# Modulation weights asked for by SyncE, modulation rounds spread by columns, and a later token-matrix store in a two-layer diffusion step

## The chip, the cores and the metric

One core of one Trainium2 chip. The metric is device microseconds of one execution of the whole program; lower is better.

## The reference, cut to what matters

Two layers, each on 1280 tokens (1024 latent, 256 prompt) of width 1024:

```python
ada = silu(cond) @ w_ada[l] + b_ada[l]            # 1024 x 6144, one row per condition
sh1, sc1, g1, sh2, sc2, g2 = split(ada, 6)
h = x * (1 + sc1) + sh1
z = h @ w_in[l]                                   # 1024 x 2816: hyena | conformer | q | k | v
y = concat(hyena(z), conformer(z), attention(rope(q), rope(k), v)) @ w_out[l]
x = layer_norm(ALPHA * x + g1 * y); h = x * (1 + sc2) + sh2
x = layer_norm(ALPHA * x + g2 * (relu(h @ w_mlp1[l]) ** 2 @ w_mlp2[l]))
```

## The kernel before, in words

Every engine has its own program, in order, tied to the others by counting semaphores. The stage at issue is the input projection, once per layer. The columns of `w_in` come as 22 blocks of 128. The first 18 blocks make z tiles, three for each block: tokens 0 to 511, 512 to 1023 and the prompt's 256 (`q` = 0, 1, 2). `Z_ORDER` numbers the 54 tiles; this number is `at`. Tiles 0 to 17 are the first six blocks, `q` outermost; from tile 18 (`Z_FIRST`) on, each block's three tiles follow one another, so that (n, 2) is tile 3n+2. Blocks 18 to 21 make ten value tiles afterwards.

- **TensorE**, `z_tile` (line 1043): waits for the block, and through `z_evac` for the tile four before to have left its PSUM bank (line 1053), multiplies (24 matmuls), and then runs what `modulation(at)` (line 1070) puts behind this tile. After value tile 0 it turns the last prompt keys (`new_keys(3)`, line 1128), which waits for the copy out of tile 53 (line 1103).
- **Modulation.** The columns of `w_ada` that are not loaded at the start are computed beside the projection in blocks of 512 columns, two *rounds* each: 24 rounds in layer 0 and 16 in layer 1, 8 matmuls a round (line 978), plus one *turn* (line 985) for each block. A round needs 1 MB of weights in `ADW`, which holds one round only, so the next round's weights can be asked for only when the round before has been computed (`ada_used`). `ada_round_at(l, r)` (line 127) says behind which tile round r lies: 3 + 2r in layer 0, 19 + 2r in layer 1. Rounds count from 0.
- **ScalarE** copies each z tile out of PSUM (lines 1764, 1772), stores it, and asks for the weights of the next round in `load_ada` (line 1651, two DMAs a round). In the same program stand the convolutions' loads and stores (`conv_load`, `conv_store`): behind tiles 18, 20, ... 30 and 42 it waits for the convolution that VectorE is computing, stores it and loads the next. For the queries and keys (blocks 10 to 17) it makes the high part of the block before (line 1691, waits for GpSimd's rotation), copies tile (n, 2), and asks for 8 DMAs that swap rows into `ZSW` (`partners`, line 1685). `ZSW` is one buffer.
- **GpSimd** splits every weight block into a high and a low part (`split`, lines 770 and 774) and rotates queries and keys (lines 809 to 813), in one order: split of block n, `split_rotated(n - 17)`, `rotate(n - 16)`.
- **SyncE** loads the weight blocks into `RAW`, two buffers: block b is asked for when block b-2 is split (`load_block`, line 594). Blocks of the next stage (`B_FWD`, "forward blocks" 0, 1, ...) follow the 22. Behind block 7 it waits for the layer's input to be final (`xs_ready`), stores the token matrix `XT` (5.2 MB, line 658), waits for that store, and loads the cached keys and the rotation table (`CKR`, `ROPE`) into the room that it leaves.

Of the kernel before, what the change touches and what calls it, by code (L numbers as in the profile page):

```python
# [2 lines left out]

# [9 lines left out]
DEPTH = 2  # L13
# [7 lines left out]
CHUNKS = [(0, 512), (512, 512), (1024, 256)]  # L21
# [14 lines left out]
B_IN, B_FWD, B_INV, B_OUT, B_MLP, BLOCKS = 0, 22, 39, 48, 56, 120  # L36
# [25 lines left out]
ADA_BLOCKS = [[(0, c) for c in range(OWN, 12)] + [(1, c) for c in range(OWN)], [(1, c) for c in range(OWN, 12)]]  # L62
# [5 lines left out]
Z_ORDER = [(n, q) for q in range(3) for n in range(FIRST_TILES)] + \  # L68
    [(n, q) for n in range(FIRST_TILES, Z_V) for q in range(3)]
Z_FIRST = 3 * FIRST_TILES  # L70
# [30 lines left out]
def spot_of(t):  # L101

    return {8: 6144}.get(t, spot(t))
# [20 lines left out]
    return max(x for x in range(at - 6, at) if down_bank(x) == down_bank(at)) + 1  # L124


def ada_round_at(l, r):

    return (3 if l == 0 else Z_FIRST + 1) + 2 * r


def ada_turn_at(l, b):
    return ada_round_at(l, 2 * b + 1) + 1
# [75 lines left out]
def program(nc, ins, consts, outs):  # L209
# [20 lines left out]
    def place(name, shape, dtype, offset):  # L230
        return nc.alloc_sbuf_tensor_at(name, shape, dtype, offset=offset)
# [24 lines left out]
    ADW = place("ADW", [128, 2, 2, 512], F32, ADW_O)  # L256
# [157 lines left out]
    with ExitStack() as ctx:  # L414
# [3 lines left out]
        def signal(name, per_layer=0, start=0):  # L418
            return Signal(ctx.enter_context(nc.semaphore(name)), per_layer, start)
# [7 lines left out]
        ada_in = signal("ada_in", 2 * ADA_MAX * 32)  # L427
        ada_used = signal("ada_used", 2 * ADA_MAX, OWN)
# [20 lines left out]
        h_ready = signal("h_ready", 48, 24)  # L449
# [122 lines left out]
        def column_block(w, l, j):  # L572

            return w[l].rearrange("(k p) n -> p k n", p=128)[:, :, bass.ts(j, 128)]
# [9 lines left out]
        def dft_columns(part, j):  # L584
            return dft_d[part].rearrange("(k p) n -> p k n", p=128)[:, :, j * 128:(j + 1) * 128]
# [7 lines left out]
        def _(sp):  # L593
            def load_block(l, b, source, view3):

                p = b % 2
                sp.wait_ge(blk_ready.sem, blk_ready.at(l, b - 1))
                to = RAW[:, p, :]
                if view3:
                    to = RAW[:, p, :].rearrange("p (k n) -> p k n", k=source.shape[1])  # L600
                sp.dma_start(to, source).then_inc(raw_in[p].sem, 16)
# [44 lines left out]
            layer_vectors(0)  # L646
            for l in range(DEPTH):

                for n in range(ZT):
                    if l or n > 1:  # L650
                        load_block(l, B_IN + n, column_block(w_in, l, COLUMNS[n]), True)
                    if l and n == 3:
                        layer_vectors(l)
                    if n == 7:

                        sp.wait_ge(xs_ready.sem, xs_ready.at(l, 0))
                        for half in range(2):
                            sp.dma_start(x_d[:, 4 * half:4 * half + 4, :], XT[:, 4 * half:4 * half + 4, :])\
                              .then_inc(x_spilled.sem, 16)
                        sp.wait_ge(h_ready.sem, h_ready.at(l, 0))  # L660
                        sp.wait_ge(x_spilled.sem, x_spilled.at(l, 2 * 16))
                        sp.dma_start(CKR[:], cache_k[0, l].rearrange("(t p) m d -> p t (m d)", p=128))\
                          .then_inc(ck_in.sem, 16)
                        sp.dma_start(ROPE[:], rope_d).then_inc(rope_in.sem, 16)
                for j in range(ST):
                    for part in range(2):
                        load_block(l, B_FWD + 2 * j + part, dft_columns(part, j), True)
                load_block(l, B_FWD + 16, dftp_d, False)

# [57 lines left out]
                for i in range(21):  # L727
                    q, j = i // 7, i % 7
# [12 lines left out]
                with sp.Fori(0, GROUPS) as g:  # L741
                    for e in range(4):
                        b = B_MLP + e
                        p = b % 2
# [739 lines left out]
        def _(act):  # L1484
# [124 lines left out]
            for l in range(DEPTH):  # L1609
# [38 lines left out]
                    act.wait_ge(pads_ready.sem, pads_ready.at(l, u - 5))  # L1648
                    S.activation(CFIN[:, 1, :], CFIN[:, 1, :], ACT.Sigmoid).then_inc(glu_done.sem, 1)

                def load_ada(r):

                    w, c = ADA_BLOCKS[l][r // 2]
                    act.wait_ge(ada_used.sem, ada_used.at(l, r))
                    for p in range(2):
                        k = 4 * (r % 2) + 2 * p
                        act.dma_start(ADW[:, p], w_ada[w].rearrange("(k p) n -> p k n", p=128)
                                      [:, k:k + 2, 512 * c:512 * c + 512]).then_inc(ada_in.sem, 16)

                def modulation(at):  # L1660

                    for b, (w, c) in enumerate(ADA_BLOCKS[l]):
                        for half in range(2):
                            r = 2 * b + half
                            if ada_round_at(l, r) == at:
                                if r + 1 < 2 * len(ADA_BLOCKS[l]):
                                    load_ada(r + 1)
                                if half:
                                    act.wait_ge(ada_used.sem, ada_used.at(l, r + 1))
                                    if b == 0:  # L1670
                                        act.wait_ge(lam_ready.sem, lam_ready.at(l, 1))
                                    S.activation(AROW[:], PS[:, 7, :], ACT.Copy).then_inc(ada_kept.sem, 1)
                        if ada_turn_at(l, b) == at:
                            act.wait_ge(ada_turned.sem, ada_turned.at(l, b + 1))
                            to = ADA[:, 4 * (c - OWN):4 * (c - OWN) + 4, :] if w == l else AD0[:, w, 4 * c:4 * c + 4, :]
                            S.activation(to.rearrange("p t v -> p (t v)"), PS[:, 7, 0:8], ACT.Copy)\
                             .then_inc(ada_placed.sem, 1)
# [75 lines left out]
                for at, (n, q) in enumerate(Z_ORDER):  # L1753
# [20 lines left out]
                    first_tiles(at)  # L1774
                    if at == Z_FIRST - 1:
                        act.wait_ge(h_ready.sem, h_ready.at(l, 0))
                    if at == ada_round_at(l, 0) - 1:
                        load_ada(0)
                    modulation(at)
                    if q == 0 and i > 1:  # L1780
                        store_low(i - 2)
# [76 lines left out]
                for n, (t, kind) in enumerate(STEPS):  # L1858
# [6 lines left out]
                    else:  # L1865
                        act.wait_ge(u_psum.sem, u_psum.at(l, FOLD_AT[t] + 1))
                        at = spot_of(t) + 256
# [275 lines left out]
            l = DEPTH - 1  # L2143
# [570 lines left out]
```

## Time and profile before

| | |
|---|---|
| median of 3 runs | 3796.18 us (3788.06 to 3804.03) |
| profiled execution | 3796.43 us |
| span of its instructions | 3794.4 us |
| mean granted TensorE clock | 0.963 of full speed |
| busy: TensorE, VectorE, GpSimd, ScalarE | 92%, 51%, 35%, 29% of the span |
| mean DMA rate over the span | 97 GB/s |

The span is what the trace shows; the execution's own time is 2.0 us longer. The projection's stretches are about 92 to 417 us (layer 0) and 1966 to 2252 us (layer 1). In a row of the trace "[t <-X]" is the time that the engine sat idle before the instruction, and what ended it; "ACTq" and "SPq" are DMA requests by ScalarE and SyncE.

### The profile page before, as it was taken

The numbers are of one execution on the slowest core, as the hardware profiler recorded it, in microseconds if no ns is written. First come the engines' busy times: TensorE is split into PE (matmuls) and PEld (weight loads), VectorE is DVE, ScalarE is ACT, GpSimd is POOL, SyncE is SP. The second block draws the span as 40 slices with busy tenths as digits, with TensorE's granted clock in tenths as the row PEclk, the third lists the DMA queues.
The fourth block names the chain that finished last, engine by engine and source line by source line (L and its number), as shares of the span: only waits on it lengthen the run. The fifth ranks groups of instructions, "written<-read, shape, count | busy, mean of one in ns | idle before, by whom it ended". The sixth has DMA issues, their size and how long they took to land. (4 is left out here: it accounts for less than half of the span.)

```text
span 3794.4 us, 48305 instructions
## 1 busy us (share of the span) xinstructions
PE 3473.6 (92%) x18386; PEld 2908.7 (77%) x18386; DVE 1949.2 (51%) x2787; ACT 1101.3 (29%) x2020; POOL 1331.2 (35%) x682
## 2 busy tenths in 40 slices
PE   6899997898899999999978899788899999999996
PEld 4677776787788888888867677577777888888885
DVE  3047665875744434444562775387674344344347
ACT  4212244672511111111242113367524111111114
POOL 3337543201533332323354474430125333323232
PEclk8999998999999999999989999899999999999998
DMA  7577646512011111111117664564201111111101
GB/s 255 213 244 230 206 124 171 134 61 81 31 38 45 34 44 35 40 39 34 34 50 252 211 211 155 160 146 120 72 21 45 34 45 34 43 36 39 39 23 56
DMA packets 285270, 368.46 MB, mean 97 GB/s; under 512 B 16887, under 2 KB 203493, under 8 KB 283782
## 3 DMA queue, kind: packets, MB, share of 16 engines
q1 hardware_dynamic: 211586, 212.63, 19.4%
q10 hardware_dynamic: 73476, 152.83, 11.8%
q8 instruction: 159, 2.61, 0.3%
q14 instruction: 49, 0.40, 0.0%
HBM read 275.48 MB, written 81.53 MB: 94 GB/s over the span
## 5 line engine op out<-in xcount | busy, mean ns | idle before, releaser
L770 POOL TENSOR_TENSOR RH<-RAW,ONE 128x1024 fp32r<-128x1024 f32 x200 | 386.9, 1934 | 1529.8 <-PE PS L929 684.5
L929 PE MATMUL PS<-HH,RH 128*128 128x512 f32 (+1 forms) x2744 | 616.1, 368 | 66.7 <-issue 25.7
L774 POOL TENSOR_TENSOR RL<-RAW,RH 128x1024 fp32r<-128x1024 f32 x240 | 578.9, 2415 | 162.3 <-ACT RH L1905 146.6
L929 PEld LDWEIGHTS PS<-HH,RH 128*128 128x128 f32 x2744 | 471.8, 195 | 187.0 <-issue 92.9
L929 PE MATMUL PS<-HL,RH 128*128 128x512 f32 (+1 forms) x2744 | 586.0, 356 | 0.0
L2555 DVE SCALAR_TENSOR_TENSOR XT<-PS,ADA,XT 128x512 f32<-128x512 f32 (+1 forms) x704 | 454.0, 663 | 244.0 <-PE PS L1421 240.4
L929 PE MATMUL PS<-HH,RL 128*128 128x512 f32 (+1 forms) x2744 | 579.1, 353 | 0.0
L929 PEld LDWEIGHTS PS<-HL,RH 128*128 128x128 f32 x2744 | 467.6, 192 | 74.2
L929 PEld LDWEIGHTS PS<-HH,RL 128*128 128x128 f32 x2744 | 460.9, 189 | 70.9
L2080 ACT ACTIVATE RB<-PS 128x512 f32<-128x512 f32 (+1 forms) x192 | 101.0, 526 | 1390.5 <-PE PS L929 1390.5
L2539 DVE TENSOR_TENSOR PS<-PS,RB 128x512 f32<-128x512 f32 (+1 forms) x192 | 117.1, 610 | 745.8 <-ACT RB L2080 745.8
L1421 PE MATMUL PS<-HBH,RH 128*128 128x512 f32 x1024 | 316.8, 391 | 3.7 <-DVE XT L2555 2.4
L1421 PE MATMUL PS<-HBL,RH 128*128 128x512 f32 x1024 | 315.6, 389 | 0.0
L1421 PE MATMUL PS<-HBH,RL 128*128 128x512 f32 x1024 | 315.4, 389 | 0.0
L2421 DVE TENSOR_REDUCE STAT<-PS 128x1 f32<-128x1280 f32 (+1 forms) x160 | 203.6, 1276 | 70.0 <-PE PS L1273 66.6
L1421 PEld LDWEIGHTS PS<-HBH,RH 128*128 128x128 f32 x1024 | 189.5, 188 | 44.9 <-DVE XT L2575 4.7
L1421 PEld LDWEIGHTS PS<-HBL,RH 128*128 128x128 f32 x1024 | 192.2, 188 | 40.4
L1421 PEld LDWEIGHTS PS<-HBH,RL 128*128 128x128 f32 x1024 | 192.2, 188 | 40.2
L2323 DVE SCALAR_TENSOR_TENSOR PS<-CFIN,VEC,PS 128x1024 f32<-128x1024 f32 (+1 forms) x232 | 206.5, 890 | 8.1
L1273 PE MATMUL PS<-KK,QH 128*128 128x512 f32 (+1 forms) x416 | 163.6, 393 | 39.6 <-ACT PB L1959 31.6
L1959 ACT ACTIVATE PB<-PS,STAT 128x1280 f32<-128x1280 f32 (+1 forms) x160 | 183.7, 1156 | 23.7 <-DVE STAT L2421 23.4
L1316 PE MATMUL PS<-V,AT 128*128 128x128 f32 x1344 | 170.4, 281 | 5.8 <-ACT OT L1989 1.3
(264 smaller groups left out, 4535.7 us busy)
## 6 DMA issues: line engine op xcount, KB each, us to landing
RAW<-in_w_mlp_dram SPq DMA_DIRECT2D x128, 512.0 KB, 3.9
ADW<-in_w_ada_dram ACTq DMA_DIRECT2D x80, 512.0 KB, 5.7
RAW<-const_dram SPq DMA_DIRECT2D x52, 512.0 KB, 4.1
RAW<-in_w_in_dram SPq DMA_DIRECT2D x44, 512.0 KB, 4.8
z_scratch<-ZST ACTq DMA_DIRECT2D x40, 256.0 KB, 3.2
x_scratch<-XT SPq DMA_DIRECT2D x4, 2560.0 KB, 12.8
QH<-q_hi SPq DMA_DIRECT2D x32, 320.0 KB, 9.4
QL<-q_lo SPq DMA_DIRECT2D x32, 320.0 KB, 10.6
```

What stands on the lines that cost most here:

```text
L770: nc.gpsimd.tensor_tensor(RH[:, s, :], RAW[:, p, :], ONE[:].broadcast_to([128, 1024]), ALU.mult)\
L774: nc.gpsimd.tensor_tensor(RL[:, s, :], RAW[:, p, :], RH[:, s, :].bitcast(F32), ALU.subtract)\
L929: mm = pe.matmul(out, w[:, s, k * 128:(k + 1) * 128], m(k), start=(n == 0 and k == 0), stop=(n == 2 and k == KT - 1))
L1273: mm = pe.matmul(PSF[:, SCORES[m] + o:SCORES[m] + o + w], qq[:, m, t * 128:(t + 1) * 128], KK[s][:, m, k0 + o:k0 + o + w], start=(x == 0), ...
L1316: mm = pe.matmul(PS[:, 7, 0:128], AT[:, g % 2, k * 128:(k + 1) * 128], V2[s][:, k0 // 128 + k, :], start=(k == 0), stop=(k == nk - 1))
L1421: mm = pe.matmul(PS[:, down_bank(m), 0:tn], w[:, slot(l, b + e), j * 128:(j + 1) * 128], x[:, e, 0:tn], start=(n == 0 and e == 0), stop=(n ...
L1959: S.activation(PB[:, g % 2, m, :kn], PSF[:, SCORES[m]:SCORES[m] + kn], ACT.Exp, bias=STAT[:, g % 4, m:m + 1], accum_out=STAT[:, g % 4, 2 + ...
L2080: S.activation(RB[:, e, :tn], PS[:, e, :tn], ACT.Relu).then_inc(relu_done.sem, 1)
L2323: C.link(V.scalar_tensor_tensor(acc if k < 30 else CFIN[:, 1, at:at + n], CFIN[:, 0, at + k:at + k + n], VEC[:, w:w + 1], acc, ALU.mult, A ...
L2421: V.tensor_reduce(STAT[:, g % 4, m:m + 1], PSF[:, SCORES[m]:SCORES[m] + kn], AX_X, ALU.max, negate=True).then_inc(smax.sem, 1)
L2539: V.tensor_tensor(up, up, RB[:, e, :tn], ALU.mult).then_inc(sq_kept.sem, 1)
L2555: V.scalar_tensor_tensor(x, PS[:, 2 + m % 6, :tn], ADA[:, A_G2 + j, COND[q]:COND[q] + 1], x, ALU.mult, ALU.add).then_inc(m2_evac.sem, 1)
```

## The change

The requests for rounds' weights move from ScalarE to SyncE. There they stand between the weight blocks: ahead of block b, SyncE asks for every round whose predecessor lies behind a tile that must be done before block b's place in the ring comes free (`freed_at`). `spread` puts the rounds at even steps of computed columns, from tile 3 (layer 0) or tile 15 (layer 1) to tile 52. The store of `XT` comes after one or two rounds' requests; the wait for its end, `CKR` and `ROPE` come after block 9 and no longer ahead of block 8. The tiles of the rounds become

```
layer 0: 3 5 7 9 11 13 17 19 21 23 25 27 30 31 34 36 38 40 42 44 46 48 51 52
layer 1: 15 19 21 24 26 28 31 33 36 38 40 43 45 48 50 52
```

```diff
+def spread(l):
+    first, n = (3, 2 * len(ADA_BLOCKS[0])) if l == 0 else (Z_FIRST - 3, 2 * len(ADA_BLOCKS[1]))
+    width = [CHUNKS[q][1] for _, q in Z_ORDER]
+    done = list(itertools.accumulate(width))
+    last = len(width) - 2
+    step = (done[last] - done[first]) / (n - 1)
+    at = [min(k for k in range(first, last + 1) if done[k] >= done[first] + step * r - 1) for r in range(n)]
+    for r in range(n - 2, -1, -1):
+        at[r] = min(at[r], at[r + 1] - 1 - r % 2)
+    return at
...
 def ada_round_at(l, r):
-    return (3 if l == 0 else Z_FIRST + 1) + 2 * r
+    return ADA_AT[l][r]
...
+                rounds_loaded = [0]
+                def load_ada(upto):
+                    while rounds_loaded[0] < 2 * len(ADA_BLOCKS[l]):
+                        r = rounds_loaded[0]
+                        if (ada_round_at(l, r - 1) if r else ada_round_at(l, 0) - 2) > upto:
+                            return
+                        w, c = ADA_BLOCKS[l][r // 2]
+                        if r == 0:
+                            sp.wait_ge(h_ready.sem, h_ready.at(l, 0 if l else -16))
+                        sp.wait_ge(ada_used.sem, ada_used.at(l, r))
+                        for p in range(2):
+                            k = 4 * (r % 2) + 2 * p
+                            sp.dma_start(ADW[:, p], w_ada[w].rearrange("(k p) n -> p k n", p=128)
+                                         [:, k:k + 2, 512 * c:512 * c + 512]).then_inc(ada_in.sem, 16)
+                        rounds_loaded[0] = r + 1
+                def freed_at(b):
+                    return Z_ORDER.index((b - 8, 2)) if b >= 8 else 2 * b - 10
+
                 for n in range(ZT):
+                    load_ada(freed_at(n))
                     if l or n > 1:
                         load_block(l, B_IN + n, column_block(w_in, l, COLUMNS[n]), True)
...
                     if n == 7:
+                        load_ada(13 if l else 8)
                         sp.wait_ge(xs_ready.sem, xs_ready.at(l, 0))
+                        sp.wait_ge(h_ready.sem, h_ready.at(l, 0))
                         for half in range(2):
                             sp.dma_start(x_d[:, 4 * half:4 * half + 4, :], XT[:, 4 * half:4 * half + 4, :])\
                               .then_inc(x_spilled.sem, 16)
-                        sp.wait_ge(h_ready.sem, h_ready.at(l, 0))
+                    if n == 9:
                         sp.wait_ge(x_spilled.sem, x_spilled.at(l, 2 * 16))
                         sp.dma_start(CKR[:], cache_k[0, l].rearrange("(t p) m d -> p t (m d)", p=128))\
                           .then_inc(ck_in.sem, 16)
                         sp.dma_start(ROPE[:], rope_d).then_inc(rope_in.sem, 16)
                 for j in range(ST):
                     for part in range(2):
+                        if 2 * j + part < 4:
+                            load_ada(freed_at(B_FWD + 2 * j + part))
                         load_block(l, B_FWD + 2 * j + part, dft_columns(part, j), True)
...
-                def load_ada(r):
...
                             if ada_round_at(l, r) == at:
-                                if r + 1 < 2 * len(ADA_BLOCKS[l]):
-                                    load_ada(r + 1)
...
-                    if at == ada_round_at(l, 0) - 1:
-                        load_ada(0)
                     modulation(at)
```

## Rows read from the trace of the kernel before

**Rows 1.** TensorE's waits, 90 to 420 us: engine line, waited for, total us, times, longest

```profile
PE PS L978 <- DMA ADW<-in_w_ada_dram: 15.5, 7, 4.2
...
PE PS L1107 <- ACT ZRAW L1772: 1.6, 1, 1.6
```

**Rows 2.** the same, 1990 to 2256 us

```profile
PE PS L978 <- DMA ADW<-in_w_ada_dram: 23.7, 8, 7.4
...
PE PS L1107 <- ACT ZRAW L1772: 2.7, 1, 2.7
```

**Rows 3.** TensorE in order of time, layer 0's value tile 0: start, us, what

```profile
411.46 2.00 PE L1120 MATMUL PS<-RH,HH 128*128 128x512 f32 x8
...
418.67 0.44 PE L1107 MATMUL PS<-IDENT,ZRAW 128*128 128x128 f32 x2 [1.58 <-ACT ZRAW L1772]
```

**Rows 4.** ScalarE in order of time, end of layer 0's projection

```profile
381.35 0.90 ACTq L1657 DMA_DIRECT2D ADW<-in_w_ada_dram  x2
...
382.35 5.10 ACTq L1685 DMA_DIRECT2D ZSW<-ZRAW  x8
...
399.48 1.28 ACT L1691 ACTIVATE ZHI<-ZRAW 128x1280 fp32r<-128x1280 f32 x1 [4.89 <-POOL ZRAW L813]
...
401.06 5.00 ACTq L1685 DMA_DIRECT2D ZSW<-ZRAW  x8
...
417.08 1.27 ACT L1691 ACTIVATE ZHI<-ZRAW 128x1280 fp32r<-128x1280 f32 x1 [7.41 <-POOL ZRAW L813]
```

**Rows 5.** GpSimd in order of time, the same stretch

```profile
392.23 2.38 POOL L809 TENSOR_TENSOR ZSW<-ZSW,ROPE 128x1024 f32<-128x1024 f32 x1 [4.29 <-DMA ZSW<-ZRAW]
...
401.38 2.39 POOL L774 TENSOR_TENSOR RL<-RAW,RH 128x1024 fp32r<-128x1024 f32 x1
...
409.81 2.41 POOL L809 TENSOR_TENSOR ZSW<-ZSW,ROPE 128x1024 f32<-128x1024 f32 x1 [3.12 <-DMA ZSW<-ZRAW]
```

**Rows 6.** ScalarE, then VectorE, in order of time, layer 0's first convolutions

```profile
202.64 1.46 ACTq L1636 DMA_DIRECT2D HYIN<-z_scratch  x3
...
216.15 0.83 ACTq L1618 DMA_DIRECT2D hyena_scratch<-CACC  x2
...
223.77 0.81 DVE L2300 TENSOR_SCALAR PS<-HYIN,VEC 128x512 f32<-128x512 f32 x1 [7.52 <-DMA HYIN<-z_scratch]
```

**Rows 7.** requests for round weights: count, ns of one request (min, median, max)

```profile
L1657 ACTq DMA_DIRECT2D ADW<-in_w_ada_dram x80: 374/490/1768, 101.8 to 2217.5; - x80
```

**Rows 8.** waits of the whole span for the loads of both rings

```profile
POOL ZSW L809 <- DMA ZSW<-ZRAW: 67.5, 16, 8.3
...
DVE PS L2300 <- DMA HYIN<-z_scratch: 61.2, 10, 7.9
```

**Rows 9.** a load of round weights that TensorE waited for: ScalarE, then TensorE

```profile
361.07 0.94 ACTq L1657 DMA_DIRECT2D ADW<-in_w_ada_dram  x2
...
368.71 1.07 PE L978 MATMUL PS<-ADW,CONDS 128*32 128x512 f32 x8 [1.51 <-DMA ADW<-in_w_ada_dram]
```

**Rows 10.** GpSimd in order of time, block 10's split in layer 0

```profile
198.95 2.39 POOL L774 TENSOR_TENSOR RL<-RAW,RH 128x1024 fp32r<-128x1024 f32 x1
```

**Rows 11.** TensorE in order of time, layer 1, after a long wait

```profile
2037.28 1.94 PE L978 MATMUL PS<-ADW,CONDS 128*32 128x512 f32 x8 [7.40 <-DMA ADW<-in_w_ada_dram]
...
2039.15 2.08 PE L929 MATMUL PS<-HH,RH 128*128 128x256 f32 x8
...
2043.93 2.00 PE L929 MATMUL PS<-HH,RH 128*128 128x512 f32 x8
```

**Rows 12.** SyncE, then GpSimd, then ScalarE in order of time, layer 1, tiles 18 to 20

```profile
2031.49 0.38 SPq L662 DMA_DIRECT2D CKR<-in_cache_k_dram  x1
...
2032.43 41.58 SPq L601 DMA_DIRECT2D RAW<-in_w_in_dram  x7
...
2047.34 1.89 POOL L770 TENSOR_TENSOR RH<-RAW,ONE 128x1024 fp32r<-128x1024 f32 x1 [34.12 <-DMA RAW<-in_w_in_dram]
...
2050.55 0.83 ACTq L1618 DMA_DIRECT2D hyena_scratch<-CACC  x2
```

More of the change, by code:

```diff
@@ L1 @@
+import itertools
 import math
@@ L124, in down_free @@
     return max(x for x in range(at - 6, at) if down_bank(x) == down_bank(at)) + 1
+def spread(l):
[8 more added lines that the diff above has]
+    return at
+ADA_AT = [spread(l) for l in range(DEPTH)]
 def ada_round_at(l, r):
-    return (3 if l == 0 else Z_FIRST + 1) + 2 * r
+    return ADA_AT[l][r]
 def ada_turn_at(l, b):
@@ L1649, in gate @@
                     S.activation(CFIN[:, 1, :], CFIN[:, 1, :], ACT.Sigmoid).then_inc(glu_done.sem, 1)
-                def load_ada(r):
[L1653 to L1658, printed above, removed]
                 def modulation(at):
```

## The prediction

> **What bounds the kernel now.** I read first who TensorE waits for in the two stretches of the projection. Weights of modulation rounds are the largest entry that the change touches: 15.5 us in 7 waits in layer 0, 23.7 us in 8 in layer 1, 39.2 us together [rows 1, 2]. It is tempting to call that the gain. But the same view has a second line: at line 1107 TensorE also waits 1.6 and 2.7 us for ScalarE's copy of a z tile, and in order of time this wait comes after the last round: value tile 0 begins at 411.46, the keys' transposes only at 418.67, when tile 53 has been copied [rows 3]. So with all those stalls in it TensorE still arrives early. Something else ends last, and a stall taken away before that point only makes this wait longer.
>
> What that is, the order of time on ScalarE and GpSimd shows. From one high part to the next (399.48 to 417.08) is a closed ring of 17.6 us: high part 1.3, the row-swap requests from 401.06 to 406.06, their landing, the rotation from 409.81, and with its end the next high part [rows 4, 5]. One ring a block, eight blocks a layer; no round weights stand in it. Ahead of it lies a second ring: convolution inputs asked for at 202.64, computed, stored and the next asked for at 216.15; VectorE sits 7.52 us idle for one of these loads [rows 6]. So the stretch from tile 18 to tile 53, 202.64 to 418, is a chain of ScalarE, VectorE, GpSimd and DMA landings, and TensorE keeps step beside it. I take this chain as the bound in both layers.
>
> **The change, part by part.** The profiled execution is 3796.4 us, within 0.3 us of the median, so the sum is made against 3796.4.
>
> *Requests leave ScalarE.* 80 requests at a median 0.49 us are 39 us of ScalarE's requesting [rows 7]. In the ring they stand beside an activation or where ScalarE waits anyway; worth zero. Another effect is worth something: a round's load in the same queue ahead of the row swaps delays them. With one asked for at 381.35 the swaps, all asked for by 387.45, were landed at 392.23, 4.8 us; without one ahead, 406.06 to 409.81, 3.75 us [rows 4, 5]. That is 1.0 us; by the spread of the loads I count two such turns a layer: **-2.0 us in each layer**. Bounds: 0 (the bytes still move) and 8 (every turn). The Trainium skill ("DMA: Bandwidth & Descriptors", section "Issuing engines are not separate DMA queues") speaks against it: requests from either engine run on the same 16 DMA engines and interleave, and a second issuer saves only issue time. By that rule the term is 0 and the sum 4 us higher; the two landings above differ in what lay ahead in one queue, which the rule leaves open.
>
> *Rounds and turns.* Their number is unchanged; 1.07 us a round stays [rows 9]. Moving them costs nothing while the chain covers them.
>
> *Requests on SyncE.* Here the change adds waits. SyncE is in order: a round's weights wait for the weight block ahead, and that for GpSimd's split. Queued behind SyncE's own waits for `ada_used` are only weight blocks whose place in the ring is not free earlier anyway: zero. The other direction costs, in three places. A late load takes 7.6 us from request to use (361.07 to 368.71) [rows 9]; after a long wait the round itself takes 1.9 us, and the next 256-wide tile 4.8 (2039.15 to 2043.93) [rows 11].
>
> 1. Layer 0, round 7 (tile 19). It stands behind block 12's request, which waits for block 10's split, done at 201.3 [rows 10]. `CKR` and `ROPE`, 1.5 MB, now lie among those blocks. Their delay is not in the trace: between 0 and 12 us (CKR, ROPE and a block, 2 MB, took 15.9 us in layer 1, 2031.49 to 2047.34 [rows 12]); I take 1.6, since blocks have slack between splits. Request 203.3, landed 210.9, round 1.9, tile 20 4.8, copy 0.4: 218.0, where ScalarE stored the first convolution at 216.15 [rows 6]. The chain moves **+1.9 us**.
> 2. Layer 0, round 23 (tile 52). By the code it stands behind forward block 2, which waits for the split that ends at 403.8 [rows 5]. Request 404.2, use 411.8, round 1.9, tile 53 4.8, turn 0.8, value tile 0 5.6 (411.46 to the wait that ended at 418.67, less 1.6 [rows 3]): 424.9 instead of 418.67, **+6.2 us**. Before, this last round's load hid behind tiles.
> 3. Layer 1, round 1 (tile 19). It stands behind block 10, block 10 behind the split of block 8, block 8 in SyncE's queue behind the token matrix, whose end was seen at 2031.49 [rows 12]. Plus 2.5 for block 8 (bounds 0 and 15.9 as above; it now has only the store ahead of it), 4.3 for its split, 0.4: request 2038.7. Landing between 7.6 and 15.9 us, with CKR, ROPE and two blocks about; I take 10, nearer the lower, since part of them has landed by then: 2048.7. Round 1.9, tile 20 4.8, copy 0.4: 2055.8, where the convolution's store stood at 2050.55: **+5.3 us** on the chain. The wait of 7.4 us at 2037.28 [rows 11] is thereby not removed but replaced by a longer one.
>
> *Token matrix.* In layer 1 it still starts when its input is final; in layer 0 it starts some 20 us later, beside rounds whose weights had slack: zero, at most one late load.
>
> The sum: layer 0 -2.0 + 1.9 + 6.2 = +6.1; layer 1 -2.0 + 5.3 = +3.3; 3796.4 + 9.4 = **3806 us**. All that is behind the projection waits for TensorE and moves along.
>
> **The rivals.**
> *A, the stalls were the bound.* All 39.2 us go, and five rounds no longer run at 1.9 instead of 1.07: -4. 3796.4 - 43 = 3753. For it: they are the largest waits. Against: the wait at line 1107 comes after them [rows 1 to 3]. Chance 0.06.
> *B, the chain gets shorter.* 16 row swaps cost GpSimd 67.5 us and 10 convolution loads cost VectorE 61.2 [rows 8]. With round weights out of ScalarE's queue each of the 26 could land 1.0 us sooner (the difference above): -26. With my late loads (+13.4) that is 3784, without them 3770; middle 3777. Against: of the two swaps shown one had no round load ahead. Chance 0.17, half of it past the bound for faster.
> *C, no leg gets shorter.* The two -2.0 fall out: 3796.4 + 13.4 = 3810. Requests only change queue, the bytes and their times stay. The section of the Trainium skill named above says the same. Chance 0.12.
> *D, slower: round weights stuck in SyncE's queue.* Place: rounds 7 and 23 in layer 0 and round 1 in layer 1, asked for right behind blocks and tables. If each takes 15.9 us instead of 7.6, 7.6 and 10, that is +8.3, +8.3 and +5.9 more: 3796.4 + 9.4 + 22.5 = 3828. It decides past 0.5% once the three together take about 10 us more than I gave them. For it: 15.9 was seen in just that queue. Against: rounds asked for beside a block took 7.6 [rows 9]. Chance 0.14.
> *E, it does not do what it says*: the even spacing is undone, since late rounds follow GpSimd's splits and not the columns. That is part of the forecast, not beside it.
>
> **How the numbers follow.** Forecast 0.51, A 0.06, B 0.17, C 0.12, D 0.14. The likeliest is mine: 3806. 0.5%, or 19 us, is about what a measurement of this kernel can tell from no change: 3777 and 3815. Faster: A and half of B, 0.14. Slower: D and 0.04 of the forecast's and C's upper ends, 0.18. The rest, 0.68, is the same. The range leaves out A and part of B below, part of D above: 3781 to 3822.
>
> **What would show it.** Right: TensorE's waits for round weights shrink in number but not at tile 19 of layer 1 and tile 52 of layer 0; the ring stays near 17.6 us; the value tiles begin some 6 and 3 us later; ScalarE's requests for `ADW` are gone. Wrong: a ring or convolution turn that is clearly shorter (B), the value tiles 15 us earlier with no wait at line 1107 (A), or SyncE asking for round 23 or round 1 before the split that I name, which would take away the two largest terms.

## The result, and the profile after

The changed kernel took 3826.03 us (median of 5 runs, 3813.43 to 3827.55) against 3798.87 us for the kernel before on the same chip: ratio 1.0071, 95% interval 1.0054 to 1.0087, that is 27 us or 0.7% slower. The forecast was 3806, with a range up to 3822. The profiled execution of the changed kernel took 3821.70 us; its span is 3819.9 us, the mean granted clock 0.959 (before 0.963). The chip read and wrote as much as before (275.48 and 81.53 MB); what changed in the queues is who asked. The page's rows for the two large DMA queues (packets, MB, share of the 16 engines):

```profile
q1 hardware_dynamic: 233346, 254.57, 22.5%
q10 hardware_dynamic: 51716, 110.88, 8.5%
```

Before, they stood at 212.63 and 152.83 MB: 42 MB, the 80 loads of 0.5 MB, went from one queue to the other, so q1 is SyncE's and q10 ScalarE's. First the waits of the whole span (waited for, total us, times, longest):

```profile
POOL ZSW L855 <- DMA ZSW<-ZRAW: 93.4, 16, 16.4
...
DVE PS L2333 <- DMA HYIN<-z_scratch: 73.4, 10, 14.5
...
PE PS L1024 <- DMA ADW<-in_w_ada_dram: 35.6, 10, 16.0
...
PE PS L1031 <- ACT AROW L1707: 27.6, 5, 9.9
```

Against [rows 8] GpSimd waits 26 us longer for row swaps and VectorE 12 us longer for convolution loads. TensorE's waits for round weights, 39.2 us before in [rows 1, 2], hardly fell; they are fewer and longer. The last row is TensorE's wait at the turn for ScalarE's copy of the row. In the kernel before it was small:

```profile
PE PS L985 <- ACT AROW L1672: 1.9, 3, 1.0
```

Second, the end of layer 0's projection, in order of time on ScalarE, SyncE, GpSimd and TensorE. It answers to [rows 3 to 5]:

```profile
410.04 1.27 ACT L1726 ACTIVATE ZHI<-ZRAW 128x1280 fp32r<-128x1280 f32 x1 [9.36 <-POOL ZRAW L859]
...
411.61 5.00 ACTq L1720 DMA_DIRECT2D ZSW<-ZRAW  x8
...
431.03 1.27 ACT L1726 ACTIVATE ZHI<-ZRAW 128x1280 fp32r<-128x1280 f32 x1 [3.47 <-POOL ZRAW L859]
...
414.33 0.37 SPq L619 DMA_DIRECT2D RAW<-const_dram  x1
414.75 1.46 SPq L682 DMA_DIRECT2D ADW<-in_w_ada_dram  x2
...
423.84 2.35 POOL L855 TENSOR_TENSOR ZSW<-ZSW,ROPE 128x1024 f32<-128x1024 f32 x1 [6.63 <-DMA ZSW<-ZRAW]
...
424.69 1.94 PE L1024 MATMUL PS<-ADW,CONDS 128*32 128x512 f32 x8 [4.34 <-DMA ADW<-in_w_ada_dram]
...
437.10 0.38 PE L1153 MATMUL PS<-IDENT,ZRAW 128*128 128x128 f32 x2
```

The ring that took 17.6 us in [rows 4] takes 21.0 here (410.04 to 431.03). GpSimd finishes a split at 414.3, SyncE is thereby free to ask for the next block, and right behind it for 1 MB of round weights. That falls among ScalarE's eight swap requests (411.61 to 416.61). The last swap lands at 423.84, 7.2 us after the last request; in [rows 4, 5] it was 3.75 us. This time, from the eighth request to the start of the rotation that waits for the swaps, is called a leg below.

The other blocks of layer 0 agree. In four of the eight, SyncE asked for round weights 3.1 to 4.3 us behind the first swap request: their legs are 5.4, 6.5, 7.1 and 7.2 us. The other four took 1.9 to 4.0 us.

The same happens to the last convolution load (SyncE, ScalarE, VectorE):

```profile
273.59 9.35 SPq L682 DMA_DIRECT2D ADW<-in_w_ada_dram  x4
...
275.22 2.18 ACTq L1682 DMA_DIRECT2D HYIN<-z_scratch  x3
...
282.77 0.55 DVE L2333 TENSOR_SCALAR PS<-HYIN,VEC 128x256 f32<-128x256 f32 x1 [8.27 <-DMA HYIN<-z_scratch]
```

Before, VectorE waited 4.14 us for this load, and now 8.27:

```profile
277.33 0.55 DVE L2300 TENSOR_SCALAR PS<-HYIN,VEC 128x256 f32<-128x256 f32 x1 [4.14 <-DMA HYIN<-z_scratch]
```

Third, layer 1 around the token matrix (SyncE, TensorE, ScalarE), which answers to [rows 11, 12]:

```profile
2030.52 0.82 SPq L702 DMA_DIRECT2D x_scratch<-XT  x2
2031.38 11.29 SPq L619 DMA_DIRECT2D RAW<-in_w_in_dram  x2
2046.62 0.37 SPq L706 DMA_DIRECT2D CKR<-in_cache_k_dram  x1
...
2053.42 0.37 SPq L619 DMA_DIRECT2D RAW<-in_w_in_dram  x1
2053.83 1.27 SPq L682 DMA_DIRECT2D ADW<-in_w_ada_dram  x2
...
2028.01 1.07 PE L1024 MATMUL PS<-ADW,CONDS 128*32 128x512 f32 x8
...
2062.19 1.94 PE L1024 MATMUL PS<-ADW,CONDS 128*32 128x512 f32 x8 [16.04 <-DMA ADW<-in_w_ada_dram]
...
2069.67 1.24 ACTq L1664 DMA_DIRECT2D hyena_scratch<-CACC  x2
```

Round 0 was done at 2029, so `ADW` was free; round 1 was asked for at 2053.8, some 25 us later, because SyncE stood behind blocks that waited for GpSimd's splits and for the token matrix. TensorE stood still for 16.0 us.

### The profile page after: what moved, and what is told of

The parts are those of the page before. It is cut to its first block and busy times, and to the rows that moved or that the text cites. A ratio compares the mean times of both kernels' runs of the same rounds, so it can differ in the third digit from the quotient of the medians.

```text
span 3819.9 us, 48306 instructions
## 1 busy us (share of the span) xinstructions
PE 3474.6 (91%) x18386; PEld 2912.5 (76%) x18386; DVE 1934.2 (51%) x2787; ACT 1099.8 (29%) x2020; POOL 1331.6 (35%) x682
## 3 DMA queue, kind: packets, MB, share of 16 engines
HBM read 275.48 MB, written 81.53 MB: 93 GB/s over the span
```

## The experiments

Each kernel was timed in five rounds against the kernel before on its chip (medians of before 3795 to 3799 us). The table gives the ratio to before with its 95% interval, and for layer 0's projection, from one profiled execution each, how much more time than before passed in three stretches: from the first projection matmul to the last hyena convolution's store ("conv"), on to the high part before tile 53 ("rings"), on to the end of the value tiles ("tail"). Where two kernels have the same program in layer 0, the three together differed by 1 to 3 us, one stretch by 3.3; smaller differences are not read. The mean granted clock alone does not set the time: the profiled executions of e6 and e8 took 3794.74 and 3794.64 us at 0.960 and 0.966.

| kernel | asks for rounds | ratio | conv | rings | tail |
|---|---|---|---|---|---|
| changed | SyncE | 1.0071 (1.0054 to 1.0087) | +6.4 | +8.5 | +4.4 |
| e1 spread only | ScalarE | 1.0015 (1.0005 to 1.0025) | -0.1 | +2.2 | +6.3 |
| e2 all but spread | SyncE | 1.0108 (1.0090 to 1.0125) | +14.1 | +7.1 | +2.7 |
| e3 late keys only | ScalarE | 1.0019 (1.0007 to 1.0030) | +8.3 | +1.3 | 0.0 |
| e4 all but late keys | SyncE | 1.0102 (1.0085 to 1.0118) | +15.2 | +8.4 | +5.3 |
| e7 SyncE only | SyncE | 1.0130 (1.0113 to 1.0148) | +14.6 | +5.1 | +1.6 |
| e8 all but SyncE | ScalarE | 1.0016 (1.0002 to 1.0031) | -0.8 | +2.3 | +6.5 |
| e5 before, small loads | ScalarE | 0.9971 (0.9957 to 0.9985) | +1.7 | -4.8 | 0.0 |
| e6 changed, small loads | SyncE | 1.0003 (0.9994 to 1.0012) | -2.7 | -2.3 | +4.3 |
| f1 two requests earlier | SyncE | 1.0070 (1.0054 to 1.0086) | +4.3 | +6.8 | +1.0 |
| f2 and held for swaps | SyncE | 1.0058 (1.0043 to 1.0074) | +7.1 | +1.8 | +3.4 |
| f3 layer 1 alone of e8 | ScalarE | 1.0009 (0.9996 to 1.0022) | +0.6 | +0.2 | 0.0 |
| f4 and behind swaps | ScalarE | 1.0018 (1.0006 to 1.0031) | +0.5 | +3.1 | +0.1 |
| g1 | layer 0 SyncE | 1.0047 (1.0030 to 1.0064) | +9.7 | +7.1 | +5.8 |
| g2 | layer 1 SyncE | 1.0023 (1.0012 to 1.0035) | -0.3 | +2.8 | +7.0 |
| g3 turns later | SyncE | 1.0072 (1.0058 to 1.0086) | +5.3 | +8.7 | +5.3 |
| g4 f1 and round 2 | SyncE | 1.0035 (1.0024 to 1.0047) | +5.0 | +5.1 | 0.0 |

**The three parts, alone and in pairs.** e1 is the kernel before with the new tiles, and ScalarE still asks:

```diff
 def ada_round_at(l, r):
-    return (3 if l == 0 else Z_FIRST + 1) + 2 * r
+    return ADA_AT[l][r]
```

> The kernel before with the new tiles for the rounds alone; ScalarE still asks for their weights, and the token matrix is stored as before (in layer 1 the first request waits besides for the layer's input, because round 0 is now ahead of tile 18). Theory (requests of SyncE that come with a weight block, right behind GpSimd's split, slow down the row swaps and convolution loads of the rings): the spacing alone costs only what lies at its end, a last round at tile 52 whose load can be asked for no sooner than behind tile 51, 3 to 6 us in layer 0 and the same or less in layer 1; 3799 plus 3 to 10 is 3802 to 3809, rings of layer 0 near 17.6 us. Rival S (the spacing itself is the loss: turns at tiles 32 and 44 wait 8 to 10 us for ScalarE's row copy, and the last round is at tile 52): nearly all of the 27 us, 3818 to 3826.

Measured: 3805.38 us. The theory holds, and the place is the named one: of layer 0's three stretches only the tail grew by more than equal programs differ by. Round 23 stands directly behind round 22's tile there, and its load does not fit into one tile.

e2 is the changed kernel with the rounds' tiles put back:

```diff
 def ada_round_at(l, r):
-    return ADA_AT[l][r]
+    return (3 if l == 0 else Z_FIRST + 1) + 2 * r
...
-                        if (ada_round_at(l, r - 1) if r else ada_round_at(l, 0) - 2) > upto:
+                        if (ada_round_at(l, r - 1) if r else 13 if l else 1) > upto:
```

> The changed kernel with the rounds put back to tiles 3 + 2r and 19 + 2r; SyncE asks, between the weight blocks, token matrix stored late. Theory: most of the loss is still here, since the requests still come right behind GpSimd's splits: the last row swap of layer 0 takes about 7 us and no longer 3.75, high part of tile 53 8 to 14 us late; without the last round behind tile 53 some 4 us a layer are saved: 3811 to 3822. Rival S (spacing): 3796 to 3803, no leg longer. Rival P (place of the token matrix): as the theory here, told apart by the next two.

Measured: 3836.54 us, above every number named. The sign is the theory's (the spacing is not the loss), the size is not: under SyncE's requests the even spacing saves about 14 us. The extra loss is in "conv", and most of it stands already at the first convolution's store: 8.3 us behind the kernel before, counted from the start of the stretch, where the changed kernel is 1.9 behind. Why was not traced.

e3 is the kernel before with the wait for the store's end and the two tables' loads moved from behind block 7 to behind block 9; the store itself stays where it was, now behind the wait for `h_ready`:

```diff
                         sp.wait_ge(xs_ready.sem, xs_ready.at(l, 0))
+                        sp.wait_ge(h_ready.sem, h_ready.at(l, 0))
...
-                        sp.wait_ge(h_ready.sem, h_ready.at(l, 0))
+                    if n == 9:
                         sp.wait_ge(x_spilled.sem, x_spilled.at(l, 2 * 16))
                         sp.dma_start(CKR[:], cache_k[0, l].rearrange("(t p) m d -> p t (m d)", p=128))\
                           .then_inc(ck_in.sem, 16)
                         sp.dma_start(ROPE[:], rope_d).then_inc(rope_in.sem, 16)
```

> The kernel before with the wait for the token matrix, the cached keys and the rotation table moved behind block 9, and nothing else; ScalarE asks at the old tiles. Theory: the rings are untouched, within 5 us of before: 3794 to 3804; in layer 1 the longest wait for round weights gets shorter or stays, since blocks 8 and 9 no longer stand behind the token matrix. Rival P (a late 1.5 MB of keys and table pushes block 10 and the first convolution): 3806 to 3816, first convolution of layer 1 stored 4 us or more later.

Measured: 3803.87 us, at the edge between the two. All of layer 0's +8.3 stands at its first convolution's store. Ahead of it TensorE waits for round 7, whose weights ScalarE asked for at 185.8, right behind the two tables (182.9 to 184.6):

```profile
196.70 1.93 PE L979 MATMUL PS<-ADW,CONDS 128*32 128x512 f32 x8 [4.98 <-DMA ADW<-in_w_ada_dram]
```

In the kernel before this round came without a wait. e4 is the changed kernel with the reverse of it, and with the store behind round 0's request alone in layer 0:

```diff
-                        load_ada(13 if l else 8)
+                        load_ada(13 if l else 1)
...
-                    if n == 9:
                         sp.wait_ge(x_spilled.sem, x_spilled.at(l, 2 * 16))
```

> The changed kernel with the wait for the token matrix, the cached keys and the rotation table put back ahead of block 8 (and round 0 of layer 0 the only one asked for ahead of the store); SyncE asks, spread rounds. Theory: the loss of layer 0 stays (about 16 us at its last high part), in layer 1 round 1 is still late: 3818 to 3830. Rival P: 10 us or more come back: 3805 to 3814.

Measured: 3831.96 us, above both forecasts, by the ratios 0.31% or 12 us more than the changed kernel. So the later tables cost 7 us where ScalarE asks at the old tiles; where SyncE asks at the new ones, they and the later store save 12 us: the parts do not add up. That left two corners of the table, e7 with SyncE's requests alone (the edits of e2 and e4 in one kernel) and e8 with everything else (e1 and e3 in one kernel):

> SyncE asks, rounds at their old tiles, token matrix, keys and table stored and loaded as before: the one part of the change that no other run has alone. From the runs so far: spread rounds take 14 us off the run with SyncE's requests and the late keys, and the early keys add 9 us to the run with spread rounds. If the parts add up this run is at 3799 + 40 + 9 or so, 3840 to 3855; if the old tiles and the early keys cost through the same wait, 3828 to 3840. Rival (SyncE's requests do no harm alone, only together with one of the others): 3797 to 3806.

> Spread rounds and late keys, ScalarE asks: all of the change but who asks. Theory: the two small losses add up, 3797 + 6 + 7: 3804 to 3814, GpSimd's wait for row swaps stays near 68 us; the difference to the changed kernel, 15 us or more, is then SyncE's. Rival: the two together already make most of the loss, 3818 to 3828.

Measured: e7 3841.36 us, the low end of the forecast for parts that add up; e8 3799.82 us, below its forecast and less than e1 and e3 added. By the ratios SyncE's asking alone costs more than the whole loss, 1.30% or 49 us; spacing and late tables give 22 us of it back. Against e8 the changed kernel loses 0.55%, 21 us, to who asks.

**Are the bytes the cost, or the order?** e5 and e6 load only 64 of 512 columns:

```diff
+                            cn = 512 if r == 0 else 64
-                            sp.dma_start(ADW[:, p], w_ada[w].rearrange("(k p) n -> p k n", p=128)
-                                         [:, k:k + 2, 512 * c:512 * c + 512]).then_inc(ada_in.sem, 16)
+                            sp.dma_start(ADW[:, p, :, 0:cn], w_ada[w].rearrange("(k p) n -> p k n", p=128)
+                                         [:, k:k + 2, 512 * c:512 * c + cn]).then_inc(ada_in.sem, 16)
```

> The kernel before, with every round but each layer's first loading only 64 of its 512 columns (7/8 of those modulation weights are left out; matmuls, requests and waits keep their number). A round's load is then there almost at once. Theory (the rings are the bound, not TensorE's waits for round weights): little comes back, the legs that run beside a round's load and one tail a layer: 3782 to 3796. Rival A of the prediction (the stalls are the bound): 39 us less, 3755 to 3765.

> The changed kernel with the same columns left out. Theory (the loss is the bytes of round weights landing beside row swaps, convolution loads and blocks, and the late landings of rounds that follow a split): the loss all but goes, within 8 us of the run before with small loads, GpSimd's wait for row swaps falls from 93 us to 75 or less. Rival O (the order is the loss: SyncE's program holds blocks and rounds behind one another, and turns wait for ScalarE's row copy, whatever the size): still 15 us or more above the run before with small loads.

Measured: e5 3782.93 us, 11 us less than before: most of rival A's 39 us were never there. e6 is 0.3%, some 12 us, above e5, and stands between the two forecasts. In layer 0 the loss is gone but for the tail of the new spacing. There the swaps were asked for, and landed, in this way (ScalarE, SyncE, GpSimd of e6):

```profile
393.03 5.00 ACTq L1720 DMA_DIRECT2D ZSW<-ZRAW  x8
...
395.78 0.37 SPq L619 DMA_DIRECT2D RAW<-const_dram  x1
396.19 1.43 SPq L683 DMA_DIRECT2D ADW<-in_w_ada_dram  x2
...
402.22 2.35 POOL L855 TENSOR_TENSOR ZSW<-ZSW,ROPE 128x1024 f32<-128x1024 f32 x1 [3.55 <-DMA ZSW<-ZRAW]
```

Requests at the same moments as in the changed kernel, an eighth of the bytes, and the swaps land 4.2 us after the last request and not 7.2. In the four blocks of layer 0 whose legs were 5.4 to 7.2 us, e6 has 3.8 to 4.2. So in layer 0's rings it is the bytes that land among the swaps; for the convolutions the run doesn't tell their bytes from the rounds' later landing. In layer 1 TensorE still waits 13.4 us at tile 19 with loads this small:

```profile
2043.40 1.93 PE L1024 MATMUL PS<-ADW,CONDS 128*32 128x512 f32 x8 [13.38 <-DMA ADW<-in_w_ada_dram]
```

There it is the order. GpSimd's total wait for swaps, 76.5 us, missed the 75 by a little.

Why do ScalarE's own requests not do the same harm? In e8 the block at the same place shows it (ScalarE, GpSimd):

```profile
402.19 5.00 ACTq L1706 DMA_DIRECT2D ZSW<-ZRAW  x8
...
407.94 1.64 ACTq L1678 DMA_DIRECT2D ADW<-in_w_ada_dram  x2
...
410.97 2.34 POOL L828 TENSOR_TENSOR ZSW<-ZSW,ROPE 128x1024 f32<-128x1024 f32 x1 [3.15 <-DMA ZSW<-ZRAW]
```

ScalarE's program puts the round's weights behind the eighth swap (or ahead of the first), never between them; 3.8 us from the last request to the use. Over e8's eight blocks of layer 0 the legs are 1.9 to 4.1 us.

**Moving requests.** f1 moves two requests up in SyncE's program; f2 holds the others back until the block's swaps are landed:

```diff
 ADA_AT = [spread(l) for l in range(DEPTH)]
+ADA_AT[0][22] = 50
...
-                        load_ada(13 if l else 8)
+                        load_ada(15 if l else 8)
```
```diff
                         sp.wait_ge(ada_used.sem, ada_used.at(l, r))
+                        if swaps > 0:
+                            sp.wait_ge(qk_partner.sem, qk_partner.at(l, swaps * 8 * 16))
```

> The changed kernel with two requests moved up in SyncE's program and nothing else: round 22 of layer 0 goes from tile 51 to tile 50, so that round 23 is asked for ahead of forward block 2's wait and not behind it; round 1 of layer 1 is asked for ahead of the token matrix. Theory (a request's place behind a split or the store is a loss of its own): layer 0's value tiles end 4 to 8 us earlier and its last leg of row swaps is back under 5 us; in layer 1 TensorE's wait of 16.0 us at tile 19 goes, the first convolution is stored 6 to 10 us earlier; together 10 to 18 us: 3806 to 3816. Rival (only the sum of bytes matters): 3820 or more.

> The same, and in the stretch of queries and keys SyncE holds a round's weights back until the row swaps of the block are landed. Theory (what lengthens the swaps' legs is a round's weights asked for by the other queue among the eight swaps): no leg over 4.7 us from the last request to the landing, GpSimd's wait for the swaps in layer 0 from 51 us to 38 or less, layer 0's last high part 6 to 10 us earlier than in the changed kernel; rounds come later, which may cost TensorE some waits that are not on the chain: 3798 to 3810. Rival (the rounds' lateness was the loss, the legs follow it): slower than the run beside it, 3815 or more.

Measured: f1 3823.19 us, no gain, against the theory's 10 to 18. It lies in the rival's range, but the rival (only the bytes matter) does not survive g4 below, where one more request is moved and no byte. In layer 0 the tail came back (+1.0 from +4.4). In layer 1 the wait had moved from round 1 to round 2 (SyncE, TensorE, ScalarE of f1):

```profile
2023.50 0.91 SPq L683 DMA_DIRECT2D ADW<-in_w_ada_dram  x2
...
2049.76 14.41 SPq L620 DMA_DIRECT2D RAW<-in_w_in_dram  x4
2064.21 1.34 SPq L683 DMA_DIRECT2D ADW<-in_w_ada_dram  x2
...
2040.44 1.07 PE L1025 MATMUL PS<-ADW,CONDS 128*32 128x512 f32 x8
...
2073.17 1.93 PE L1025 MATMUL PS<-ADW,CONDS 128*32 128x512 f32 x8 [18.14 <-DMA ADW<-in_w_ada_dram]
...
2082.75 0.60 ACT L1800 ACTIVATE ZST<-PS 128x512 f32<-128x512 f32 x1 [18.59 <-PE PS L976]
...
2083.77 0.92 ACTq L1665 DMA_DIRECT2D hyena_scratch<-CACC  x2
```

Round 1 is done at 2041.5, round 2 is asked for at 2064.2, behind four blocks. The last two rows show how such a wait reaches the chain: ScalarE waits 18.59 us for the next z tile, and the convolution's store is behind that copy in its program.

f2 took 3818.64 us, above its forecast. Its mechanism holds in the main: "rings" fell from +6.8 to +1.8, and the block at the same place landed 4.3 us after its last request (one leg of layer 0 still took 6.2, with weights asked for 1.4 us behind its first swap; GpSimd's wait for swaps there is 43.8 us, not 38, of which the first block's wait alone is 16.0; in the changed kernel it is 16.3). But the rounds came later for it, the tail grew by 2.4 us and "conv" by 2.8 (it has no hold there; that is within what equal programs differ by), and against f1 the medians can't be told apart.

f3 and f4 were made for speed. f3 is e8 in layer 1 and the kernel before in layer 0; f4 asks for the round's weights behind the block's eight swaps wherever it asked ahead of them.

```diff
+                                    if q == 2 and i >= 0:
+                                        late.append(r + 1)
+                                    else:
                                         load_ada(r + 1)
...
                         partners(i)
+                        while late:
+                            load_ada(late.pop())
```

> ScalarE asks; layer 0 is as in the kernel before; layer 1 has the spread rounds and the late keys. In the run with both parts and ScalarE asking, layer 1's projection took 388.7 us against 399.3 before, and layer 0's 394.9 against 386.8. Theory: the two layers can be had apart, 3796 - 10.6: 3782 to 3789. Rival (that layer 1 gain was one execution's luck): 3792 to 3798.

> The same, and in the tiles that ask for row swaps ScalarE asks for the round's weights behind the eight swaps and not ahead of them. Theory (in one engine's program, what is asked for first lands first): legs with a round's load ahead go from 4.4 to 4.7 us to 3.3 to 3.9, some 1 us each in three or so legs a layer: 2 to 6 us less than the run beside it, 3778 to 3786. Rival (the rounds' later request costs as much): the same or slower than the run beside it.

Measured: 3800.44 and 3802.23 us; the theory fell in both, and f3 is a little above its rival's range too. A gain of 10 us that one execution showed in layer 1 did not stand in the medians, and where ScalarE puts the load, ahead of the swaps or behind, made no difference clear of the noise. No kernel tried here beats the one before, save with most of the weights left out.

**Which layer loses how much.** g1 and g2 let ScalarE ask in one layer (g1 in layer 1, g2 in layer 0 with `l == 0`; ScalarE's requests there are those of e8). g3 puts three turns a tile later; g4 is f1 with one more request moved up:

```diff
                 def load_ada(upto):
+                    if l == 1:
+                        return
```
```diff
-    return ada_round_at(l, 2 * b + 1) + 1
+    return ada_round_at(l, 2 * b + 1) + (2 if (l, b) in ((0, 6), (1, 3), (1, 5)) else 1)
```
```diff
                         sp.dma_start(ROPE[:], rope_d).then_inc(rope_in.sem, 16)
+                        if l:
+                            load_ada(19)
```

> The changed kernel, with ScalarE asking in layer 1 alone (layer 0 still SyncE). By the profiled executions so far, SyncE's asking costs layer 0's projection 11 us (406.2 against 394.9 with the same rounds) and layer 1's 11 us (399.5 against 388.7). Theory (each layer loses about half, each by its own mechanism): 3809 to 3817, TensorE's longest wait for round weights in layer 1 under 8 us. Rival (all of it is layer 0's, the layer 1 wait is off the chain): 3822 or more.

> The changed kernel, with ScalarE asking in layer 0 alone (layer 1 still SyncE). Theory: 3809 to 3817, row swaps in layer 0 landed within 4.8 us of the last request, TensorE's 16 us wait at tile 19 of layer 1 unchanged. Rival (all of it is layer 1's): 3822 or more; if all is layer 0's: 3800 to 3805.

> The changed kernel with the turns behind the rounds at tile 31 (layer 0), 33 and 43 (layer 1) one tile later. TensorE waited 8.4, 8.1 and 9.9 us there for ScalarE's row copy. Theory (TensorE was early there, the rings are the bound): the three waits shrink by half or more, the time by 0 to 6 us: 3820 to 3828. Rival (the turns are what costs): 3800 to 3812.

> The run with two requests moved up, with round 2 of layer 1 asked for right behind the rotation table as well. Theory (the wait stuck in SyncE's program is on the chain of layer 1 by its convolutions): TensorE's longest wait for round weights in layer 1 falls from 18.1 us to under 8, the second convolution's store in layer 1 5 to 8 us earlier than there, 3823 less 5 to 9: 3813 to 3819. Rival (it moves on to round 3 once more): no change, 3820 to 3827.

Measured: g1 3813.52, g2 3808.85, g3 3823.86, g4 3807.67 us; the theory held in g1 and g3, and g2 lies 0.15 us under its range. Both layers lose, layer 0 more: giving it back to ScalarE brings 0.48%, 18 us, and layer 1 0.24%, 9 us, each with about 0.2% of uncertainty, so that layer 1's part is only just clear of it. g3: TensorE's waits for the row copy got shorter (9.3 to 4.1 us in all in layer 0, 18.3 to 4.2 in layer 1), others grew in their place (in layer 1, 7.7 us for the copy behind the turn and 6.4 for a z tile's), and the time stayed: TensorE was early there. g4 bears on layer 1 (SyncE, TensorE):

```profile
2037.53 0.94 SPq L683 DMA_DIRECT2D ADW<-in_w_ada_dram  x2
...
2050.36 1.06 PE L1027 MATMUL PS<-ADW,CONDS 128*32 128x512 f32 x8 [1.67 <-DMA ADW<-in_w_ada_dram]
...
2072.70 1.94 PE L1027 MATMUL PS<-ADW,CONDS 128*32 128x512 f32 x8 [5.55 <-DMA ADW<-in_w_ada_dram]
```

One request, asked for 3.2 us behind round 1's start and not 23.8 as in f1, took the 18 us wait away, no wait for round weights above 5.5 us came in its place, and the ratio fell from 1.0070 to 1.0035: 13 us. It came out better than forecast.

The traces show less of this gain than the medians. Counted from the start of the stretch, layer 1's second convolution was stored 6.1 us earlier than in f1, as forecast, but the end of the value tiles only 3.2 us earlier: layer 1's projection took 347.7 us in g4's profiled execution, 350.9 in f1's, 347.6 in the changed kernel's and 339.5 before. By the three stretches of the table, layer 1 lost +4.6, +2.7 and +0.8 us in the changed kernel, +2.5, +5.2 and +0.4 in g4, and -0.3, -2.1 and +0.1 in e8. So SyncE's asking costs layer 1 in its "rings" too, g4's edit does not bring that back, and where the rest of the 13 us was gained these executions do not show. Slow swaps do not explain the changed kernel's "rings" in layer 1: one leg there is above 4 us, 4.4.

## Why the prediction was wrong

The reading of the bound was right in the main: TensorE's waits for round weights are not it (e5 got 11 of their 39 us back), and in layer 0 they hardly changed in sum (15.5 before, 17.1 after) while its "rings" grew with the row swaps' legs. But a wait of TensorE counts where ScalarE's next copy stands behind it, as at tile 19 of layer 1, and at the end of layer 0. Four steps after that went wrong, the second and third only in part.

1. **"Requests leave ScalarE: -2.0 us in each layer"** has the wrong sign. It was read from one leg with a round's load ahead of the swaps (4.8 us) and one without (3.75), and held the shared queue to be the cause. What the trace showed there was the good case: in ScalarE's program a load can stand ahead of the swaps or behind them. The ring it read as free of round weights, 399.48 to 417.08, is so because the last round, at tile 49, was over by then. SyncE asks when a split ends, which in this ring is while the swaps are being asked for: legs of 5.4 to 7.2 us where that happens. "Rings" went to +8.5 us in layer 0 where the same rounds asked for by ScalarE give +2.3, and "conv" to +6.4 where they give -0.8: in place of -2.0 us, some 12 to 15 more in these two stretches of layer 0 (changed kernel and g1 against e8 and g2).

   The Trainium skill ("DMA: Bandwidth & Descriptors", section "Issuing engines are not separate DMA queues") was the better guide: requests of different engines run on the same 16 DMA engines and interleave, and a second issuer saves only issue time. The runs agree with the first half, 7.2 us against 3.8. They go further than the second: who asks was worth 21 us (e8 against the changed kernel). For layer 0's legs and layer 1's tile 19 the rows show how: by the moment at which SyncE's program lets the request go.

2. **Round 1 of layer 1.** Mechanism and local size were right. The stretch starts 15.8 us later than before (1981.70 against 1965.91); with that, the request was forecast for 2054.5 and came at 2053.8, its landing took 8.4 us against 10, and the first convolution's store moved by +3.3 us against +5.3. What the sum left out is that the same program holds every round of that stretch behind blocks, and that ScalarE's in-order copies hand the wait on to the convolutions. Moving round 1 alone changed nothing (f1); with round 2 moved too 13 us came back in the medians (g4), of which the traces place 3.2 in this stretch.

3. **"Rounds and turns: moving them costs nothing while the chain covers them."** For the turns it held (g3), although their waits of 8 to 10 us were not foreseen. For the last round it did not: the tail is +6.3 to +7.0 us where ScalarE asks at the new tiles (e1, e8, g2), and 0.0 where it asks at the old ones (e3). The term of +6.2 us for round 23 was the right size, and its cause was wrong: not SyncE's place behind forward block 2, but two rounds on neighbouring tiles at the end, whoever asks. In the changed kernel `ADW` came free at 413.7, and SyncE asked at 414.75: its place cost 1 us.

4. **"Token matrix: zero", and 1.6 us for the late tables.** Late tables alone cost 7 us (e3, where the store itself is not later); together with the later store they save 12 beside SyncE's requests (e4 against the changed kernel). The store's place alone was not run. Each part was costed by itself; the prediction weighed no pair of parts.

Round 7 of layer 0 was asked for at 200.9 and used at 210.2, forecast 203.3 and 210.9; its +1.9 us is there at the first convolution's store, counted from the start of the stretch (+4.3 in g1, the same program), and down to +0.6 at the third. Rival D, at 3828, was nearest to the measured time and named the right queue, but its number is near by luck: it priced three landings of 15.9 us each, and they took 9.3, 9.9 and 8.4. What stays open: of layer 0's "conv" loss only the last load was read from rows (4.1 us of 6.4); layer 1's "rings" have no cause shown; and the layers' parts (18 and 9 us against the changed kernel, 12 and 3 against e8) add up only within their uncertainty.

## What to carry to other kernels

When a load moves to another engine's program, ask at which moments that program will let it go, and what is landing then; here a request behind a semaphore wait was let go just while the critical transfers were being asked for. Read the whole stretch of an in-order program for what stands behind its waits, not the first late request alone: taking one away showed the next here. Parts of a change that meet on one queue are to be costed in pairs.

## What was not expected of the hardware

One eighth of a load's bytes, asked for at the same moment from the other queue, cut the landing of eight small transfers from 7.2 to 4.2 us behind their last request; the same 1 MB asked for by the transfers' own engine behind them left it at 3.8.
